# Seven half-size products for eight in the mixing and second feed-forward products of a two-block sequence model

## The reference

```
mix = concat(retention, pooling, forgetting attention)   # 528 x 1024
h = layer_norm(ALPHA * h + mix @ w_out)                  # w_out 1024 x 1024
a, b = h @ w1, h @ w3                                    # 1024 x 2816 each
h = layer_norm(ALPHA * h + (silu(a) * b) @ w2)           # w2 2816 x 1024
```

## Time and profile before

| | us |
|---|---|
| median of 3 runs (3255.95 to 3266.2) | 3258.08 |
| profiled execution, span from its first to its last instruction | 3252.7 |
| TensorE matmul busy in the span | 3120.2 (96%) |
| VectorE busy | 975.8 (30%) |
| ScalarE busy | 540.8 (17%) |
| GpSimd busy | 47.2 (1%) |
| layers, 1728 to 3253 us of the span: TensorE busy | 1500.70 of 1525 |

### The profile page before, as it was taken

How to read it: one execution, slowest core, us unless ns; L and a number is a source line. 1 busy time by engine, 2 the same in 40 slices (tenths; PEclk the granted TensorE clock), 3 DMA queues, 4 the chain that set the end, 5 groups by cost and what they waited for, 6 DMA issues and landing times.

```text
span 3252.7 us, 52666 instructions
## 1 busy us (share of the span) xinstructions
PE 3120.2 (96%) x22631; PEld 1747.5 (54%) x22631; DVE 975.8 (30%) x2146; ACT 540.8 (17%) x1129; POOL 47.2 (1%) x58
## 2 busy tenths in 40 slices
PE   9878989999999999999999999999999999999999
PEld 3355545333343333333345668574785758675866
DVE  1633455232223223222363431223023122132101
ACT  1332311111111111111122220130102100040000
POOL 0000002000000000000010000000000000000000
PEclk9888979999999999999989999999999999999999
DMA  9800115999999999999863333234333243243532
GB/s 400 354 1 27 53 53 224 386 410 403 408 397 406 400 406 407 407 407 404 351 251 119 125 130 117 111 143 176 135 126 142 105 194 133 100 176 116 195 145 100
DMA packets 97466, 743.70 MB, mean 229 GB/s; under 512 B 11128, under 2 KB 38336, under 8 KB 57552
## 3 DMA queue, kind: packets, MB, share of 16 engines
q1 hardware_dynamic: 58768, 687.49, 53.6%
q10 hardware_dynamic: 32624, 30.52, 2.9%
q0 software_dynamic: 5968, 24.14, 1.9%
HBM read 674.98 MB, written 67.13 MB: 228 GB/s over the span
## 4 chain that ended last, share of the span: by engine, by line
PE 55%; DMA 28%; DVE 3%; ACT 2%; issue 1%; ACTq 1%; POOL 0%; DVEq 0%
DMA arena<-x_sorted 27%; PE psum L1593 19%; PE psum L1610 9%; PE psum L1540 5%; PE psum L1579 3%; PE psum L1551 3%; PE psum L1244 1%; PE psum L802 1%; ACTq L587 1%; PE psum L1355 1%; PE psum L820 1%; PE psum L1196 1%; PE psum L1319 1%; PE psum L1411 1%; PE psum L1457 1%
## 5 line engine op out<-in xcount | busy, mean ns | idle before, releaser
L1244 PE MATMUL psum<-weight_ring,arena 128*32 128x512 f32 x6192 | 680.8, 594 | 23.6 <-DVE arena L2862 21.7
L1593 PE MATMUL psum<-arena,weight_ring 128*128 128x256 f32 (+1 forms) x2816 | 632.2, 383 | 3.1 <-ACT arena L2226 3.1
L1593 PEld LDWEIGHTS psum<-arena,weight_ring 128*128 128x128 f32 x2816 | 527.6, 189 | 99.0 <-issue 11.0
L1244 PEld LDWEIGHTS psum<-weight_ring,arena 128*32 128x32 f32 x6192 | 199.7, 110 | 485.5 <-issue 464.3
L1319 PE MATMUL psum<-weight_ring,arena 128*32 128x256 f32 x6144 | 338.2, 380 | 0.0
L1610 PE MATMUL psum<-weight_ring 128*128 128x512 f32 x704 | 305.4, 593 | 4.2 <-DVE weight_ring L3149 4.2
L1319 PEld LDWEIGHTS psum<-weight_ring,arena 128*32 128x32 f32 x6144 | 196.6, 110 | 153.0 <-issue 26.8
L1610 PEld LDWEIGHTS psum<-weight_ring 128*128 128x128 f32 x704 | 132.9, 190 | 169.3 <-issue 162.5
L2884 DVE STREAM_TRANSPOSE arena<-arena 128x384 f32<-128x384 f32 x32 | 18.6, 580 | 630.8 <-DMA arena<-x_sorted 630.8
L3149 DVE TENSOR_TENSOR weight_ring<-weight_ring,psum 128x256 f32<-128x256 f32 (+1 forms) x88 | 37.5, 426 | 486.1 <-PE psum L1593 480.3
L1540 PE MATMUL psum<-weight_ring,arena 128*128 128x512 f32 (+2 forms) x512 | 170.0, 489 | 3.1 <-ACT arena L2226 3.1
(11 more groups left out here) (435 smaller groups left out, 2532.0 us busy)
## 6 DMA issues: line engine op xcount, KB each, us to landing
weight_ring<-exp_gu SPq DMA_DIRECT2D x129, 2048.0 KB, 11.9
weight_ring<-weights SPq DMA_DIRECT2D x104, 2048.0 KB, 7.8
weight_ring<-exp_down SPq DMA_DIRECT2D x64, 2048.0 KB, 11.5
x_sorted<-arena SPq DMA_DIRECT2D x2, 10752.0 KB
arena<-x_sorted ACTq DMA_DIRECT2D x132, 96.0 KB, 21.6
y_sorted<-arena ACTq DMA_DIRECT2D x128, 96.0 KB, 17.6
y_sorted<-arena SPq DMA_DIRECT2D x2, 5632.0 KB, 39.7
y_sorted<-arena SPq DMA_DIRECT2D x2, 5120.0 KB, 37.3
```

The costliest lines, as they stand in the source:

```text
L1244: mm = pe.matmul(psum[j * GROUP:(j + 1) * GROUP, g, :], xg[:, k // 4, g, k % 4 * GROUP:(k % 4 + 1) * GROUP], w[:, kk, j * 512:(j + 1) * 51 ...
L1593: mm = pe.matmul(bank[:, 0:b - a], w[:, k, col:col + P], h2_t[:, k, a:b], start=(k == 0), stop=(k == KT - 1))
```

## The change

Both products now go through one routine, `fast`, in 16 units (`FAST`): four of mix (depth 4 tiles, twice) and twelve of feed_down, whose chunks are now 8, 8 and 6 hidden tiles (depth 4, 4, 3, twice). In a unit the two row tiles ("first" and "t") are the two halves of the left matrix's rows, the two weight pieces b1x and b2x the halves of the depth, and the two 512-column halves those of the result. Instead of the eight products of half size it makes seven (Strassen's scheme in Winograd's form), with differences on both sides:

- VectorE, on the left side: s1, the difference that overwrites the rows of "first", s2, s4 (each 128 x 512, or 128 x 384 at depth 3), and one of the four weight differences, b11 = b22 - t1 (128 x 2048).
- GpSimd, on the weights: t1 = b12 - b11, b12 = b22 - b12 (in two halves), b21 = b21 - b11 (each 128 x 2048 or 128 x 1536).
- ScalarE: a copy of the first product out of PSUM (`fast_u2`).
- VectorE, on the result: nine adds of 128 x 512 where there were four.

TensorE's order in a unit is [meta], P1, P7, P2, P6, P5, P4, P3, each of `depth` matmuls of 512 columns. P7 waits for the first two left differences and for t1 and both halves of b12; P2 for ScalarE's copy; P6 for b11; P5 for its bank; P4 for b21 and for VectorE's reading of P7's bank; P3 for VectorE's reading of P5's bank. Attention steps stand ahead of P1, P2, P5 and P3 (`STEP_SLOTS`), and ahead of meta in feed_down. Core of the diff:

```diff
-FF_CHUNKS = ((0, 12), (12, FT))
+FF_CHUNKS = ((0, 8), (8, 16), (16, FT))
+STEP_SLOTS = (0, 2, 4, 6)
# TensorE, in fast()
+                product(bank_p1, lambda k: rows(k, t), b11).then_inc(part_filled, 1)
+                bank_p7 = main.reserve(pe, 2)
+                pe.wait_ge(sums_ready, 7 * u + 2)
+                pe.wait_ge(diffs_ready, 4 * u + 3)
+                product(bank_p7, lambda k: rows(k, first), b12).then_inc(part_filled, 1)
...
+                ready_late(P)
+                pe.wait_ge(part_copied, u + 1)
+                mm = product(bank_p1, lambda k: rows(depth + k, t), b21, False)
+                main.ship(mm, ("fast", u, "c11"), "v")
...
+                bank_p6 = main.reserve(pe, 0)
+                pe.wait_ge(sums_ready, 7 * u + 5)
+                mm = product(bank_p6, lambda k: fast_s2[:, k, :], b11)
...
+                product(bank_p5, lambda k: fast_s1[:, k, :], fast_t1).then_inc(part_filled, 1)
...
+                pe.wait_ge(diffs_ready, 4 * u + 4)
+                pe.wait_ge(sums_ready, 7 * u + 6)
+                mm = product(bank_p7, lambda k: rows(depth + k, first), b21, False)
...
+                pe.wait_ge(sums_ready, 7 * u + 7)
+                mm = product(bank_p5, lambda k: fast_s4[:, k, :], b22, False)
# GpSimd, for each unit
+                if u:
+                    pool.wait_ge(part_filled, 3 * u)
+                pool.tensor_tensor(fast_t1[:, 0:depth, :], b12, b11, ALU.subtract).then_inc(diffs_ready, 1)
+                if u in fast_meta:
+                    pool.wait_ge(*fast_meta[u])
+                for part in (slice(0, depth // 2), slice(depth // 2, depth)):
+                    pool.tensor_tensor(b12[:, part, :], b22[:, part, :], b12[:, part, :], ALU.subtract).then_inc(diffs_ready, 1)
+                pool.wait_ge(sums_ready, 7 * u + 5)
+                main.take(pool, ("fast", u, "c11"))
+                pool.tensor_tensor(b21, b21, b11, ALU.subtract).then_inc(diffs_ready, 1)
# VectorE, in fast()
+                then(dve.tensor_tensor(s1, rows(0, first), rows(1, first), ALU.add), sums_ready)
+                V.did(dve.tensor_tensor(rows(0, first), rows(0, t), rows(0, first), ALU.subtract), sums_ready)
+                then(dve.tensor_tensor(s2, s1, rows(0, t), ALU.subtract), sums_ready)
+                V.did(dve.tensor_tensor(s4, rows(1, t), s2, ALU.subtract), sums_ready)
...
+                then(dve.tensor_tensor(b11, b22, t1, ALU.subtract), sums_ready)
...
+                add(t, 1, main.take(dve, ("fast", u, "c12")), 1.0, main.drained["v"])
+                V.settle()
+                if ready is not None:
+                    norm_scaled(centered, ready, parts)
+                    half_stats(t, 1)
+                    norm_scaled(norm_centered(t), ready, parts)
+                    if has_meta(l, x):
+                        half_stats(0, 0)
+                        half_stats(0, 1)
+                        norm_scaled(norm_centered(0), ready, parts)
...
-    nc = bacc.Bacc("TRN2", target_bir_lowering=False, num_devices=1)
+    nc = bacc.Bacc("TRN2", target_bir_lowering=False, num_devices=1, dynamic_dma_scratch_size=4096)
```

More of the change, by code:

```diff
@@ L594, in build @@
         expert_landed = [sem(f"expert_landed_{k}") for k in range(6)]
-        landed2 = [sem(f"late_weights_landed_{k}") for k in range(SLOTS)]
+        landed2 = {k: sem(f"late_weights_landed_{k}") for k in (3, 4, 5)}
         slot_free2 = {}
@@ L733, in project_items, with operand_from @@
             yield "forget", 0, None
-        def rows_items(l, x):
-            for half in range(2):
-                for t in WHOLE[x]:
-                    yield half, t
-            if 0 in rows_of(l, x):
-                yield None, 0
+        def operand_from(name, l, x):
+            return 0 if name == "mix" else span(l, x)[0]
         def fox_tiles(x, unit):
@@ L2316, in layers @@
                 steps = attend(1, "B")
-                feed_up(1, "A", 0, steps)
-                feed_down(1, "A", 0, steps)
-                feed_up(1, "A", 1, steps)
+                for c in range(LAST_CHUNK):
+                    feed_up(1, "A", c, steps)
+                    feed_down(1, "A", c, steps)
+                feed_up(1, "A", LAST_CHUNK, steps)
                 each(steps, PLANS["B"].steps)
+                mix(1, "B")
                 roots(3, 4)
-                last = feed_down(1, "A", 1, none, True)
+                last = feed_down(1, "A", LAST_CHUNK, none, True)
                 turn_rows("mid", 1, "B", (last,))
@@ L3207, in feed @@
+            def feed_down(l, x, c, steps, landed=None):
+                end = sem("layer_start") if c == LAST_CHUNK else None
+                fast(FAST.index(("down", l, x, c)), ff_t, steps, end, landed, 2 if l == LAYERS - 1 else 1)
             def feed(l, x, steps, landed):
-                for c in range(2):
+                for c in range(len(FF_CHUNKS)):
                     feed_up(l, x, c, steps)
@@ L3230, in layers @@
                 steps = attend(1, "B")
-                feed_up(1, "A", 0, steps)
-                feed_down(1, "A", 0, steps)
-                feed_up(1, "A", 1, steps)
+                for c in range(LAST_CHUNK):
+                    feed_up(1, "A", c, steps)
+                    feed_down(1, "A", c, steps)
+                feed_up(1, "A", LAST_CHUNK, steps)
                 each(steps, PLANS["B"].steps)
                 mix(1, "B", 5)
-                feed_down(1, "A", 1, none, 6)
+                feed_down(1, "A", LAST_CHUNK, none, 6)
                 feed(1, "B", none, 6)
```

347 lines of the change are left out of this document (230 added, 117 removed), and 3 rows, old and new, of the table FAST.

## The result

The change made the kernel slower: 3275.99 us median of 10 runs (3267.72 to 3283.49) against 3263.87 (3255.95 to 3269.31) of the kernel before on the same chip; ratio 1.0038, interval 1.0027 to 1.0049. The forecast was 3239, 19 us under the time before, in a range of 3224 to 3264. It came 12 us over the time before, and 12 over the top of the range.

A forecast was written before the change was run, and what follows sets the result against it. TensorE's matmuls were taken to bound the layers. Savings of 52.0 + 2.2 less costs of 17, 10.5, 2, 2, 2 and 1.6 gave 19 us, so 3258.08 became 3239, range 3224 to 3264.

The forecast's parts named there:

- What is added, where it is hidden: In each unit: VectorE's 11.3 us fit under TensorE's 24.3, and GpSimd's 4.2 us b21 hides under P6 and P5.
- rival A: GpSimd and VectorE exclude each other at joins, b21 and attention steps: 12 to 13 us, time 3252; chance 0.25.
- terms 3 and 5: Units with meta: b12 late behind meta, 2 us; attention steps: less time and VectorE shared with adds, 2 us (0 to 8).
- Term 2, the clock: TensorE's clock drops to 1.2 GHz behind each of three waits where units follow norms: 3.5 us each, 10.5 us.
- The removal's worth: In mix and feed_down, 60 matmuls of 0.867 us go, shortening the layers one for one: 52.0 us.
- Term 1, the joins: Three places where a unit follows straight on norms: TensorE waits 8.1, 3.9 and 4.5 us for VectorE, 17 with gaps.
- Term 6, the tail: At the end, the scaling of "first" comes after the last product: 1.6 us.
- The 2.18 us wait: Wait at 2450.89 in the kernel before, from a heavy attention step that now falls elsewhere: 2.2 us saved.
- The scratch: Smaller DMA scratch, touching the 32 indirect DMAs: 0 us, up to 10.
- Term 4: Four more entries into feed_down at 0.53 us each: 2 us.
- the signs named ahead: Three TensorE waits for VectorE in units' second products, longest 8 us in mix(0,B); wrong if absent or in most units.
- right by A: Sign for rival A: VectorE instructions far over their 0.69 or 1.29 us beside a GpSimd one.

The follow-up runs named there:

- tiny: Changed kernel with GpSimd's three differences in every unit but the first on 8 of 512 columns (wrong results): layers 1509.2 us, ratio 0.9961 to the kernel before.
- both: Changed kernel with norms run inside the next unit, GpSimd's differences in four pieces each, additions from PSUM: layers 1507.7 us, ratio 0.9952 to the kernel before.
- owed: Changed kernel with the norms at three places run inside the next unit, behind its first differences: layers 1523.9 us, ratio 0.9988 to the kernel before.
- fewer: Kernel before with 60 matmuls of 512 columns left out of its products (terms missing in the output): layers 1476.8 us, ratio 0.9853.
- waits: Kernel before with three added waits of TensorE for the norms ahead of mix(0,B), mix(1,A) and feed_down (1,A)'s second chunk: layers 1548.2 us, ratio 1.0072.
- scratch: Kernel before with only dynamic_dma_scratch_size=4096 set, a smaller DMA scratch: layers 1522.4 us, ratio 1.0001.
- chunks: Kernel before with the feed-forward in three chunks of 8, 8 and 6 instead of 12 and 10, products whole: layers 1525.4 us, ratio 1.0006.
- tinyowed: Changed kernel with norms run inside the next unit and GpSimd's differences on 8 of 512 columns, first unit excepted (wrong results): layers 1492.6 us, ratio 0.9888.

## Why the prediction was wrong

**The step that failed** is the paragraph "What is added, where it is hidden". It took VectorE's work in a unit as 11.3 us under 24.3, each instruction at its own price, and so hidden. But the pieces of these eleven microseconds have points by which they must be through, and GpSimd holds VectorE's instructions with SBUF operands for up to 4.5 us each time. This is rival A, given 0.25. Its mechanism was right and its size was not: it put 12 to 13 us, and *tiny* shows 29.5 for all that GpSimd costs; of that, 16.2 came back when GpSimd kept all its work and only the holding was eased (*both* against *owed*, by the layers). What A missed: the last product waits for additions that GpSimd's t1, begun for the next unit, holds (3.33 twice); t1 or b12 holds sums and the scalings of attention steps (2.33, 2.10, 3.87, 2.45), where terms 3 and 5 together had 4 us and measured 12.3; and many such waits bring the clock with them. The Trainium skill ("SBUF — State Buffer", "Who interferes with whom") says that whoever issues first keeps the shared ports for its whole instruction and the other is fully blocked; the trace agrees (6.23 for 1.90, ending one addition behind GpSimd), and by it A should have been the forecast, though its 3252 was too low as well.

**Term 2, the clock,** put 3.5 us at each of three waits. At those three it measured 8.2 for 10.5, so the price was somewhat high; but six more stretches at 0.50 cost 14.8, and they had no term. One of them, 1.7 us at the layers' start, isn't the change's. I had taken from one row that 2.18 us of idle leave the clock alone; in *fewer* and *waits* the same wait was followed by 0.66 over 5 us.

**The removal's worth.** 52 was counted as a gain one for one "as long as nothing new makes TensorE wait". At full clock, busy time fell by 49.5 here and by 51.2 in *fewer*, and *fewer* as a whole gave 45.6: shorter products uncovered the additions behind them and a stretch of lower clock.

**Terms that held.** GpSimd's 2048 elements took 4.52 (forecast 4.2), VectorE's 2.29 (2.3). Term 1, the joins, measured 18.5 for 17. That the norms' queue makes them is shown by *owed*, which removes them, and by *tiny*, where they are 18.1 without GpSimd. Term 6, the tail, was 1.9 for 1.6: from TensorE's last matmul to the end of the span it took 7.1 us before and 9.0 after. The 2.18 us wait is gone, as counted. The scratch costs nothing. Term 4 was near by luck: *chunks* came to 3.0 for 2, but only 0.5 of it is waiting.

The account in idle and clock: forecast idle 22.4 (17 + 2 + 2 + 2 + 1.6 - 2.2), measured 42.8; forecast clock 10.5, measured 23.0; removed 52.0, measured 49.5. 20.4 + 12.5 + 2.5 = 35 us, which is the distance from -19 to +16. Of the 42.8, the joins are 18.5, the last products 6.7, the units with meta 5.1, the attention steps 7.2, the tail 1.9, and 1.7 are a wait of L1714 behind the third join (2.76 for 1.11); less the 2.2 saved these are 38.9, and the rest lies in gaps too short to list.

That GpSimd and the joins' norms are the causes is shown by *tinyowed*, which takes 46.1 away, and by its first unit, left whole, which holds 9.7 of the 12.8 that stay. How GpSimd's 29.5 split between what it holds and its own lateness is not shown: *tiny* shortens both at once.

By the signs named ahead: the three waits were there and VectorE's instructions were far over their prices, so "right by A" applied, and the time was beyond what A allowed (3262). Waits of over 0.6 us stood in eight of the sixteen units, at the edge of "most".

## What to carry to other kernels

Work put beside a dense engine has two prices: its own, and that of everything that it holds. Before moving elementwise work to GpSimd, list VectorE's instructions with SBUF operands that can fall beside it, cut GpSimd's part into pieces about as long as one of them, and try giving VectorE's urgent ones an operand in PSUM (here that took waits away in the trace, but no time that the runs could show). In these traces most new waits of TensorE of two microseconds and more cost themselves and 1.7 to 3.1 us of clock besides, so count the waits, not only their sum.

## What the runs showed of the hardware

The exclusion works by the instruction: four GpSimd pieces of 1.3 us hold an addition by about one of them, one of 4.5 holds it by all of that. It hits VectorE's tensor_scalar from SBUF too (4.58 us for 0.77), and spares forms with one operand in PSUM, which stayed at 0.69. Where both streams are dense each slows the other (1.7 for 0.69, 1.8 for 1.27), and together they are about as long as one after the other: four sums and four pieces, 2.8 + 5.1 us alone, took 7.7.

The same wait of 2.18 us left the clock at 1.00 in both profiles of the kernel before (*scratch* is the second) and was followed by 0.66 over 5 us in *fewer* and *waits*, which differ elsewhere. The same waits at the layers' start, 1.62 and 1.97, left it at 1.00 in twelve profiles and were followed by a stretch at 0.50 in five, with the same instructions before and behind them. And in *chunks* such a stretch came 3 us behind a wait of only 0.51. Whether a short wait costs the clock isn't settled by its length.
